# PEER diffusion step on one core: 64 gathered latent tokens with 448 dense columns, and gate matrices in loads of 16 blocks

## What is computed

```python
q = (xb @ w_pq).reshape(TOK_BLOCK, PEER_HEADS, 2, D_KEY_HALF)
s = jnp.einsum('thcd,hcnd->thcn', q, sub_keys)
s1, i1 = lax.top_k(s[:, :, 0], PEER_TOPK)
s2, i2 = lax.top_k(s[:, :, 1], PEER_TOPK)
...
top_s, pos = lax.top_k(cand_s, PEER_TOPK)
eidx = jnp.take_along_axis(cand_i, pos, axis=-1)
g = jax.nn.softmax(top_s, axis=-1)
a = jax.nn.gelu(jnp.einsum('thkd,td->thk', jnp.take(u_exp, eidx, axis=0), xb))
return jnp.einsum('thk,thkd->td', g * a, jnp.take(v_exp, eidx, axis=0))
```

## Time and profile before

| | |
|---|---|
| median of 3 runs | 3987.83 us (3984.5 to 3989.89) |
| the profiled execution | 3981.41 us, span 3979.6 us |
| TensorE (PE) matmuls busy | 3838.0 us, 96% |
| DVE busy | 2916.1 us, 73% |
| ACT busy | 1673.6 us, 42% |
| POOL busy | 2279.5 us, 57% |
| granted clock of TensorE, mean | 0.987 |
| moved by DMA | 972.44 MB, mean 244 GB/s |

### The profile page before, as it was taken

The page is one execution under the profiler, slowest core; times in us unless marked ns, Lnnn a source line. Parts: engine busy times, 40 slices in busy tenths (PEclk is TensorE's granted clock), DMA queues, the critical chain, the costliest instruction groups (busy, mean ns, idle before and its releaser), DMA issues.

```text
span 3979.6 us, 57585 instructions
## 1 busy us (share of the span) xinstructions
PE 3838.0 (96%) x21170; PEld 3355.6 (84%) x21170; DVE 2916.1 (73%) x4499; ACT 1673.6 (42%) x2920; POOL 2279.5 (57%) x1240
## 2 busy tenths in 40 slices
PE   7978899999999999999989989999999999999998
PEld 5756898888888888888879989888888888888886
DVE  4775218899875499999983320889987549999997
ACT  3265323556666422223231131355666643222322
POOL 1101224666666688888842222467666668888884
PEclk8999999999999999999999999999999999999999
DMA  5302324788888899999954312378888889999995
GB/s 209 129 2 81 127 85 138 264 281 305 302 302 308 313 342 317 330 319 327 335 181 175 117 54 90 131 257 285 300 302 300 311 314 341 314 327 322 321 333 185
DMA packets 396808, 972.44 MB, mean 244 GB/s; under 512 B 32160, under 2 KB 221344, under 8 KB 382880
## 3 DMA queue, kind: packets, MB, share of 16 engines
q1 hardware_dynamic: 301664, 630.72, 46.9%
q0 software_dynamic: 92160, 335.59, 22.7%
q10 hardware_dynamic: 2752, 3.21, 0.2%
HBM read 835.37 MB, written 133.96 MB: 244 GB/s over the span
## 4 chain that ended last, share of the span: by engine, by line
PE 57%; issue 26%; POOL 12%; DVE 4%; DMA 1%; DVEq 1%; ACT 0%; POOLq 0%; ACTq 0%
PE PS L775 30%; PE PS L763 18%; PE PS L565 5%; POOL SL L445 5%; POOL ROWS L452 4%; POOL SL L436 3%; PE PS L755 3%; DVE ROWS L1262 1%; PE PS L716 1%; DVE OH L1251 1%; DMA ROWS<-u_exp,EI 1%; DVE PO L1188 0%; DVE TS L1183 0%; DVE ABF L1218 0%; PE PS L548 0%
## 5 line engine op out<-in xcount | busy, mean ns | idle before, releaser
L445 POOL TENSOR_TENSOR SL<-RW,SH 128x1024 fp32r<-128x1024 f32 x512 | 1333.2, 2604 | 728.6 <-ACT SH L989 715.4
L989 ACT CAST SH<-RW 128x1024 fp32r<-128x1024 f32 x512 | 537.2, 1049 | 1430.3 <-PE PS L775 826.5
L763 PE MATMUL PS<-HH,SH 128*128 128x480 f32 x2048 | 799.6, 390 | 5.5 <-POOL SL L445 4.2
L775 PE MATMUL PS<-WH,SH 128*128 128x480 f32 x2048 | 777.0, 379 | 2.2 <-ACT GE L995 1.3
L763 PE MATMUL PS<-HH,SL 128*128 128x480 f32 x2048 | 776.5, 379 | 0.0
L763 PE MATMUL PS<-HL,SH 128*128 128x480 f32 x2048 | 776.3, 379 | 0.0
L775 PE MATMUL PS<-WH,SL 128*128 128x480 f32 x2048 | 775.2, 379 | 0.0
L775 PE MATMUL PS<-WL,SH 128*128 128x480 f32 x2048 | 775.1, 378 | 0.0
L436 POOL TENSOR_TENSOR SL<-RW,SH 128x1024 fp32r<-128x1024 f32 x84 | 202.6, 2416 | 808.3 <-ACT SH L820 808.3
L1312 DVE TENSOR_TENSOR WL<-GL,WH 128x480 fp32r<-128x480 f32 x256 | 558.6, 2182 | 20.6 <-ACT WH L1028 17.4
L1251 DVE TENSOR_TENSOR OH<-PS,PK 128x1024 f32<-128x1024 f32 x240 | 291.5, 1220 | 221.7 <-PE PS L755 207.7
(11 more groups left out here) (171 smaller groups left out, 5225.5 us busy)
## 6 DMA issues: line engine op xcount, KB each, us to landing
RW<-u_blk SPq DMA_DIRECT2D x256, 512.0 KB, 4.5
RW<-v_blk SPq DMA_DIRECT2D x256, 512.0 KB, 5.9
gate_acts<-GE SPq DMA_DIRECT2D x256, 240.0 KB, 3.2
router_weights<-GT SPq DMA_DIRECT2D x60, 1024.0 KB, 5.0
GB<-router_weights SPq DMA_DIRECT2D x32, 1920.0 KB, 14.5
GL<-gate_acts SPq DMA_DIRECT2D x256, 240.0 KB, 5.5
RW<-wstream SPq DMA_DIRECT2D x100, 512.0 KB, 4.3
AW<-wpairs SPq DMA_DIRECT2D x40, 1024.0 KB, 4.9
```

The source lines that it names most:

```text
L445: nc.gpsimd.tensor_tensor(SL[:, r % 2], RW[:, r % RAW], SH[:, r % 2].bitcast(F32), ALU.subtract).then_inc(raw_used, 1)
L763: last = mm(PS[:, n % 2, NG:NS], w[:, n % 2, j], a[:, j, NG:NS], start=(j == 0 and q == 0), stop=(j == DJ - 1 and q == 2))
L775: last = mm(PS[:, dj, NG:NS], w[:, k % 2, dj], a[:, k, NG:NS], start=start, stop=stop)
L989: nc.scalar.copy(SH[:, r % 2], RW[:, r % RAW]).then_inc(hi_done, 1)
```

## The change

NG goes from 32 to 64: 64 latent tokens are gathered (GQ = 2 copies with PG = 64 rounds, NPICK = 192) and 448 computed densely (112 quads). GROUP goes from 8 to 16: a load of gates covers 16 blocks. GB is twice as large, so GB0 moves from BIG to X, and, being longer than X, over the one-hot buffer OH behind it. X's return from memory then waits until DVE has used GB0. PICK_AT spreads 192 picks, with 11, 27, 42, 42 and 70 for 9, 21, 36, 36 and 58. FOLD gets columns of its own.

```diff
-GROUP = 8
+GROUP = 16
...
-NG = 32
+NG = 64
...
-PICK_AT = (_spread(20, 28, 9) + _spread(28, 45, 21) + _spread(45, 68, 36) + _spread(68, 91, 36)
-           + _spread(91, 127, NPICK - 102))
+PICK_AT = (_spread(20, 28, 11) + _spread(28, 45, 27) + _spread(45, 68, 42) + _spread(68, 91, 42)
+           + _spread(91, 127, NPICK - 122))
...
-    GB = [sb(f"GB{k}", [P, NTG, GROUP, TG], F32, at=at)[0] for k, at in enumerate((at_BIG + 16384, at_HH))]
+    GB = [sb(f"GB{k}", [P, NTG, GROUP, TG], F32, at=at)[0] for k, at in enumerate((at_X, at_HH))]
...
-    FOLD = CO[:, C_SEL:C_SEL + NG]
+    FOLD = CO[:, C_FOLD:C_FOLD + NG]
...
-                if n % GROUP == GROUP - 1 and n + 9 < NB_E:
-                    load_gates((n + 9) // GROUP)
-                if n == NB_E - 16:
+                if n % GROUP == GROUP - 1 and n + GROUP + 1 < NB_E:
+                    load_gates((n + GROUP + 1) // GROUP)
+                if n == NB_E - GROUP:
+                    sp.wait_ge(w_done, (l + 1) * NB_E - GROUP)
                     sp.dma_start(X[:], x_dram).then_inc(x_back, 16)
```

More of the change, by code:

```diff
@@ L92 @@
 QUADS_AT = [[g for g in range(NQ) if QUAD_BLOCK[g] == n] for n in range(NB_E)]
-PICK_AT = (_spread(20, 28, 9) + _spread(28, 45, 21) + _spread(45, 68, 36) + _spread(68, 91, 36)
-           + _spread(91, 127, NPICK - 102))
+PICK_AT = (_spread(20, 28, 11) + _spread(28, 45, 27) + _spread(45, 68, 42) + _spread(68, 91, 42)
+           + _spread(91, 127, NPICK - 122))
 VPICK_AT = _spread(2, NB_E, NPICK)
-C_MEAN, C_HEAD, C_SWAP, C_ID, C_IOTA, C_SEL, C_COS, C_SIN = 0, 128, 256, 384, 512, 640, 672, 1184
-C_ALL = 1696
+C_MEAN, C_HEAD, C_SWAP, C_ID, C_IOTA, C_SEL, C_FOLD, C_COS, C_SIN = 0, 128, 256, 384, 512, 640, 648, 712, 1224
+C_ALL = 1736
 def hybrid_step(nc, xT, cond, consts, wstream, wpairs, bada, gains, hgain, convp, kcache, vcache, subk,
@@ L1476, in _constants @@
     c[:, C_IOTA:C_IOTA + NKEY] = np.arange(NKEY)
-    for s in range(32):
+    for s in range(2):
         c[:, C_SEL + s] = p % 32 == s
+    for t in range(NG):
+        c[:, C_FOLD + t] = p % NG == t
     axis = HD // 2
```

## The result

The changed kernel takes 4084.61 us (4081.97 to 4088.65, three runs), the kernel before 3987.83. The ratio is 1.0245, with a 95% interval of 1.0222 to 1.0268: slower by 2.4%. Slower was forecast, but by 20 us, and it is 97; the range ended at 4060.

What follows compares the result with a forecast made beforehand. TensorE was taken as the bound, with DVE and POOL close behind in the v stage. Terms of -27.6 (u), +30 (v) and +8 (loads) gave +10.4 us a layer, +21 in all: forecast 4008 us, range 3945 to 4060.

Steps and rivals of the forecast that it cites:

- What bounds the kernel now: Whole kernel: TensorE busy all the time in each window; in the v stage it leads DVE by 0.04 us a block.
- Parts 1 and 2: Dense products: 32 columns fewer save 14.0 ns each, 172 us in all; 8 quads fewer a layer save 7.1 us.
- Part 3: u stage: 32 picks more a layer, with the savings in columns and quads, give -27.6 us a layer (ends -50 and -17).
- where TensorE decides: u blocks 91 to 127, within the u-stage sum: TensorE sets the pace, so narrower products give -12.4 us.
- Part 4: v stage: 32 row updates more make DVE's chain longest, 5.5 us a block taken between 5.43 and 5.54; +30 us a layer.
- Part 5: Gate loads, 8 of 3584 KB for 16 of 1920 KB: RW comes late, +8 us a layer (ends 0 and +27).
- Part 6: GB0's move to X and OH, SP's wait for w_done, two partition groups, 20 KB more constants: no cost.
- the saving wins: Rival: v cadence 5.42 us or less, so v's loss is below u's gain; -15 a layer, 3958 us; chance 0.22.
- TensorE remains the bound: Rival: TensorE stays the bound everywhere, -172 - 14, about 3802 us; chance 0.05.
- the draw: Rival: the v stage's loss equals the u stage's gain, 3988 us; chance 0.12.
- the cheap column: Rival: products follow columns by a third of 0.4375 ns only, u gains 8 us a layer; 4048 us; chance 0.02.
- the loads decide: Rival: bytes count, RW over 3 us late at each of 8 loads, 27 us a layer; 4046 us; chance 0.03.

Runs made afterwards that it cites:

- e5: e1_group8 with POOL's subtraction in the v stage over only half of the weights (low parts of the other half stale): 3888.04 us, ratio 0.9762.
- e3: The kernel before with dense products 448 columns wide for 480, nothing else changed: 3925.73 us, ratio 0.9856.
- e1_group8: The changed kernel with its 64 gathered tokens but gates in 16 loads of 8 blocks, GB0 back in BIG: 4044.46 us, ratio 1.0155.
- e2: The kernel before (32 gathered tokens, 480 dense columns) with gates in 8 loads of 16 blocks, 3840 KB each: 4035.23 us, ratio 1.0135.
- e7: The changed kernel with each gate load cut into four, issued in successive blocks, first GL loads behind them one a block: 4027.48 us, ratio 1.0109.
- e4: The changed kernel with 32 of the 192 row updates of each v stage narrowed to 8 elements: 4018.06 us, ratio 1.0088.

## Why the prediction was wrong

**What bounds the kernel now** held: TensorE first, DVE and POOL taking turns right behind it. e5 shows the turn-taking, e3 how close it was. But the balance was read too kindly. In the v stage TensorE was said to lead by 0.04 us a block, 5 us in all; in e3 narrower products gave 1.4 us, 0.01 a block. And "TensorE is busy all the time in each" was taken to mean that it leads in each, but in e3 blocks 28 to 44 gain nothing from narrower products.

**Parts 1 and 2, columns and quads.** 14.0 ns a product: right in the u stage, measured 14.0; in the v stage it is 11 (216.9 to 205.7 ns in e5), and the difference cost nothing, as DVE is the last there. The quads weren't tried alone. TensorE's busy time fell by 86 us (3838.0 to 3751.9), not by the 170 that the profile after was to show.

**Part 3, the u stage: -27.6 taken, -15.8 measured (e1_group8).** Three of its terms were near: -10.5 measured for the first 28 blocks (-12.7 taken), -5.5 for 68 to 90 (-6.5), -0.6 for 45 to 67 (+4, too pessimistic: a pick against SBUF was priced at 1.71 us, the mean of 20 of them, and averages 1.54 in e1). Blocks 28 to 44 became 4.5 us longer, where 0 was taken and +3 was the upper end. The largest error is the last part, "where TensorE decides": -3.4 for -12.4. DVE was indeed idle enough there, but the part ends in the seam, and 8 us of TensorE's new leisure went into a wait for RW. The step failed because only DVE was asked whether it could follow, and not the queue. (The upper ends of this part add up to -16, not -17; it changes nothing.)

**Part 4, the v stage: +30 taken, +48 measured.** The mechanism, the alternation of 6.09 and 5.13, was read from the right rows and stands in the trace after to 0.03 us. The step that failed is the choice "I take 5.5, between two numbers": 5.43 came from adding a quarter of an update to a mean, which takes for granted that work can be averaged over blocks. The order of the instructions was known, so the 5.54 was the only number that belonged to it. Of the 18 us that were missing the choice of 5.5 is 5 us, and another 4 are the 0.03 between 5.54 and the measured 5.57. The 6 us for a start ahead weren't there. The last 3 are the order again: 66 of the 126 blocks have two updates, and not half of them.

**Part 5, the loads: +8 taken, +20 measured** (5 in u, 15 in v). The landing was right, 20.4 for 20, and so was the place. At the load of 1457.30 RW also came when it was to come, after 22.4 us for 21 to 23. What failed is the other side of the sum, "RW is needed 22 us after the GB load was issued". It rests on "the next RW load, issued 3.8 us later", read in a kernel in which SP waits for freed buffers (for POOL's subtraction 440.5 us in 111 waits of the v stage; 242.9 in 73 with the change). With the change SP issues RW 0.5 us behind the load, the issue takes 11.2 us, and ACT needs the weights 16.6 us after the load, so that it waits 5.8 us where 0.5 to 1 were put down. The GL loads behind RW were not counted; in e2 DVE waits 31.0 us for them. At the seam, 1 to 3 us were taken. TensorE waits 12.3 there, of which 8.0 stand in part 3, as e1 has them with the small loads; the large ones add the rest. e7 shows that the burst is the cost, not the bytes.

**Part 6** held as far as is known: e7 keeps GB0 in X and SP's wait for w_done, and is still 17 us faster than e1, which has neither. The move wasn't tried alone.

Per layer that is -15.8 + 47.9 + 20.3 = 52.4 for the 10.4 taken; twice that is 105 us of the 107 between the two spans. All three errors lie on one side, and the range was cut at 4060 because the upper ends "together are unlikely". They weren't independent: each takes for granted that a queue or engine with little room left has room for the average.

**The rivals.** That the saving wins, that TensorE remains the bound, the draw and the cheap column are all out. That the loads decide was half right: they are 40 of the 97 us.

## What to carry to other kernels

In the v stage TensorE was busy 99.9% and DVE 95%, and DVE was a bound all the same: ask of each cut what the second one does at the new pace, and if DVE and POOL both read two SBUF tensors, add their times before you compare. Where work comes in lumps (one update or two a block), cost the actual order of the blocks, not the mean: the same 192 updates in another order gave 28 us. And a big transfer ahead of small urgent ones in one queue costs by how long they stand behind it; cut it into pieces and put them a block apart.

## What was not expected of the hardware

- Issuing a DMA can block its queue for long: the RW load behind a load of 3584 KB of gates took SP 11.2 us to issue (4.46 behind the smaller one), and four GL loads of 224 KB behind the first such load 21.2 us.
- In e2 the loads of 3840 KB land after 20.5 us, in the kernel before those of 1920 KB after 14.5, 187 and 132 KB a microsecond, beside the same other traffic. The larger load, with packets twice as long, was quicker by the byte, and it cost time nevertheless. (Size and packets aren't parted: e7's 896 KB in the long packets take 12.2 us.)
- With the turn-taking gone (e5) the DMA engines run at a share of 0.99 and 356 GB/s in the v stage, while TensorE sets the pace: there is no room left on them either.
- A DVE instruction's time depends on where its second operand lies: a pick of 128x1024 takes 1.22 us against PSUM whether POOL subtracts beside it or not, and against SBUF 1.22 without POOL and 2.12 beside it (e1). Even an update of 8 elements took 2.65 us beside POOL (e4).
